# Expert weight rows dealt to partitions in 8 KB runs, with strided slices in the transposes that match them

## What is computed

```
for e in range(N_EXPERTS):
    h = jax.nn.silu(xf @ w_gate[e]) * (xf @ w_up[e])
    y = y + combine[:, e:e + 1] * (h @ w_down[e]).astype(jnp.float32)
```

## Time and profile before

| | |
|---|---|
| median of three executions | 643.84 us |
| profiled execution, span | 643.9 us |
| MoE on PE, from the first transpose of a gathered tile to the last matmul | 241.2 to 557.7 us |
| one step of the loop | 17.9 us |
| busy: PE, DVE, ACT, POOL | 92%, 80%, 56%, 31% |
| read from HBM, written | 147.90 MB, 14.41 MB |

### The profile page before, as it was taken

One profiled execution on the slowest core, in us unless ns is written; L12 is line 12 of the kernel. 1 busy time (PEld: TensorE's weight loads), 2 busy tenths in 40 slices (PEclk: granted clock), 3 DMA queues, 4 the chain that ended last, 5 costly groups with the idle time before them and its releaser, 6 DMA issues.

```text
span 643.9 us, 9840 instructions
## 1 busy us (share of the span) xinstructions
PE 593.1 (92%) x3432; PEld 512.1 (80%) x3432; DVE 512.3 (80%) x555; ACT 362.7 (56%) x369; POOL 198.7 (31%) x202
## 2 busy tenths in 40 slices
PE   3799999989999889799999999999999999459994
PEld 2799999968788777688888888888888888359993
DVE  4769998995633587889999999999999998387545
ACT  6712222426434526687777777778777877334343
POOL 8063635982000007422211222222221311122104
PEclk9799999979999899999999999999999999869997
DMA  9986221035131408699999999999999999480003
GB/s 255 282 255 242 66 67 66 1 140 183 57 152 66 148 30 254 248 397 394 398 396 385 389 381 362 383 379 371 387 386 366 378 376 326 154 294 3 1 1 147
DMA packets 79065, 153.99 MB, mean 239 GB/s; under 512 B 8411, under 2 KB 26419, under 8 KB 78579
## 3 DMA queue, kind: packets, MB, share of 16 engines
q1 hardware_dynamic: 71627, 138.98, 60.8%
q0 software_dynamic: 5520, 9.56, 4.0%
q10 hardware_dynamic: 1888, 5.05, 2.2%
HBM read 147.90 MB, written 14.41 MB: 252 GB/s over the span
## 4 chain that ended last, share of the span: by engine, by line
PE 70%; DMA 12%; DVE 5%; POOL 4%; ACT 3%; SPq 2%; issue 2%; POOLq 0%; ACTq 0%; DVEq 0%
PE pair L1626 19%; PE pair L1627 18%; PE pair L1628 18%; PE pair L1673 8%; DMA raw<-in_w_exp_gate 6%; PE pair L1637 3%; DMA raw<-in_w_exp_down 2%; ACT hi L826 2%; DVE lo L1174 2%; PE pair L1861 1%; DMA two<-normed,gidx 1%; SPq L459 1%; POOL h L681 1%; POOL h L683 1%; DMA two<-in_state_conv 1%
## 5 line engine op out<-in xcount | busy, mean ns | idle before, releaser
L1626 PE MATMUL pair<-hi,act_hi 128*128 128x512 f32 (+3 forms) x748 | 275.6, 369 | 7.2 <-DVE act_lo L1467 2.9
L1174 DVE TENSOR_TENSOR lo<-raw,hi 128x2048 fp32r<-128x2048 f32 x111 | 251.8, 2291 | 31.1 <-ACT hi L826 30.3
L1627 PE MATMUL pair<-lo,act_hi 128*128 128x512 f32 (+3 forms) x748 | 268.6, 359 | 0.0
L1628 PE MATMUL pair<-hi,act_lo 128*128 128x512 f32 (+3 forms) x748 | 268.6, 359 | 0.0
L826 ACT ACTIVATE hi<-raw 128x2048 fp32r<-128x2048 f32 x119 | 225.5, 1916 | 51.4 <-PE pair L1673 23.2
L1626 PEld LDWEIGHTS pair<-hi,act_hi 128*128 128x128 f32 (+1 forms) x748 | 139.5, 187 | 33.8 <-issue 5.7
L1628 PEld LDWEIGHTS pair<-hi,act_lo 128*128 128x128 f32 (+1 forms) x748 | 139.4, 186 | 22.3
L1627 PEld LDWEIGHTS pair<-lo,act_hi 128*128 128x128 f32 (+1 forms) x748 | 139.6, 187 | 19.1
L737 POOL DMA_INDIRECT pairs<-two,sidx x17 | 42.5, 2500 | 108.2 <-DVE two L1475 108.2
L1220 DVE SCALAR_TENSOR_TENSOR pair<-conv,vecs,pair 128x512 f32<-128x512 f32 x112 | 74.8, 746 | 0.0
L826 ACT ACTIVATE act_hi<-pair 128x1024 fp32r<-128x1024 f32 (+3 forms) x50 | 38.3, 782 | 58.5 <-PE pair L1637 33.3
(11 more groups left out here) (217 smaller groups left out, 512.3 us busy)
## 6 DMA issues: line engine op xcount, KB each, us to landing
raw<-in_w_exp_gate SPq DMA_DIRECT2D x34, 1024.0 KB, 10.5
raw<-in_w_exp_up SPq DMA_DIRECT2D x34, 1024.0 KB
raw<-in_w_exp_down SPq DMA_DIRECT2D x34, 1024.0 KB, 11.9
h<-in_x_prompt SPq DMA_DIRECT2D x8, 512.0 KB, 6.4
raw<-in_w_in SPq DMA_DIRECT2D x8, 512.0 KB, 12.0
raw<-in_w_in SPq DMA_DIRECT2D x4, 1024.0 KB, 9.1
raw<-in_w_out SPq DMA_DIRECT2D x4, 1024.0 KB, 4.9
raw<-in_w_ple_gate SPq DMA_DIRECT2D x4, 1024.0 KB
```

The source lines that it names most:

```text
L1174: nc.vector.tensor_tensor(lo[:, n % SPLIT, :], raw[:, n % RAW, :], hi[:, n % SPLIT, :].bitcast(F32), ALU.subtract).then_inc(lo_dve, 1)
L1626: mm(out_, x_hi, w_hi, start=start, stop=False)
L1627: mm(out_, x_hi, w_lo, start=False, stop=False)
L1628: return mm(out_, x_lo, w_hi, start=False, stop=stop)
```

## The change

The source of an expert's unit is viewed differently, so that partition p of a unit takes consecutive rows of the matrix: four for gate and up (rows 4p to 4p + 3 of the unit's 512), two for down. These are 8 KB in one piece. The unit is the same 1 MB of memory as before, in the same buffer, at the same place of SP's order. Chunk c of a gate or up unit now holds the rows 4p + c, so the token row must be cut in the same way: `dealt_rows` transposes, for chunk c, the elements 4n + c of the unit's half of the row, a slice whose elements are four floats (16 bytes) apart. For `hid` they are two floats (8 bytes) apart. The number, size and order of the transposes and matmuls stay as they were.

```diff
@@ unit_source
             if k < 4:
                 w = a["w_exp_gate"] if k < 2 else a["w_exp_up"]
-                w = w[0].rearrange("e (c p) n -> (e c) p n", p=P)
-                at = e * DC + (k % 2) * (DC // 2)
-                return w[bass.ds(at, DC // 2)].rearrange("c p n -> p c n")
-            w = a["w_exp_down"][0].rearrange("e (c p) n -> (e c) p n", p=P)
-            at = (e - 1) * CB + (k - 4) * 2
-            return w[bass.ds(at, 2)].rearrange("c p n -> p c n")
+                w = w[0].rearrange("e (u p c) n -> (e u) p (c n)", u=2, p=P)
+                return w[bass.ds(e * 2 + k % 2, 1)].rearrange("o p m -> (o p) m")
+            w = a["w_exp_down"][0].rearrange("e (u p c) n -> (e u) p (c n)", u=2, p=P)
+            return w[bass.ds((e - 1) * 2 + k - 4, 1)].rearrange("o p m -> (o p) m")
@@ load_unit
-                sp.dma_start(raw[:, n % RAW, :].rearrange("p (c n) -> p c n", c=src.shape[1]), src)\
-                  .then_inc(raw_in[n % RAW], 16)
+                to = raw[:, n % RAW, :]
+                if n < N_MOE or n >= N_GATE:
+                    to = to.rearrange("p (c n) -> p c n", c=src.shape[1])
+                sp.dma_start(to, src).then_inc(raw_in[n % RAW], 16)
...
@@ tensor
+            def dealt_rows(src, to, per):
+
+                dealt = src.rearrange("r (u n c) -> r u c n", n=P, c=per)
+                for i in range(src.shape[1] // P):
+                    ins = tr(to[:, i * P:(i + 1) * P], dealt[:, i // per, i % per, :], ident[:, :])
+                return ins
...
@@ transpose_gathered
-                transpose_rows(xg, P, pair[1]).then_inc(g_ps, 1)
+                dealt_rows(xg, pair[1], DC // 2).then_inc(g_ps, 1)
@@ transpose_hidden
-                for c in range(CB):
-                    ins = tr(bank[4][:, c * P:(c + 1) * P], hid[:, c * P:(c + 1) * P], ident[:, :])
-                ins.then_inc(t_ps, 1)
+                dealt_rows(hid, bank[4], CB // 2).then_inc(t_ps, 1)
```

More of the change, by code:

```diff
@@ L527, in _ @@
                     for i, name in enumerate(("w_exp_gate", "w_exp_up", "w_exp_down")):
-                        c = CB // 2 if i == 2 else DC // 2
-                        src = a[name][0].rearrange("e (c p) n -> (e c) p n", p=P)
+                        src = a[name][0].rearrange("e (u p c) n -> (e u) p (c n)", u=2, p=P)
                         for k in range(2):
@@ L534, in _ @@
                             sp.wait_ge(*low_done(n))
-                            sp.dma_start(raw[:, n % RAW, :].rearrange("p (c n) -> p c n", c=c),
-                                         src[bass.ds(e * 2 * c + k * c, c)].rearrange("c p n -> p c n")).then_inc(v_w[i], 16)
+                            sp.dma_start(raw[:, n % RAW, :],
+                                         src[bass.ds(e * 2 + k, 1)].rearrange("o p m -> (o p) m")).then_inc(v_w[i], 16)
                     wait_all(sp, (v_gu, j))
@@ L2021, in _ @@
                     wait_all(pe, (v_in, 16 * j))
-                    transpose_rows(xg, P, pair[1]).then_inc(v_gps, 1)
+                    dealt_rows(xg, pair[1], DC // 2).then_inc(v_gps, 1)
                     wait_all(pe, (v_gsb, j))
@@ L2030, in _ @@
                     wait_all(pe, (v_hid, j))
-                    for c in range(CB):
-                        ins = tr(bank[4][:, c * P:(c + 1) * P], hid[:, c * P:(c + 1) * P], ident[:, :])
-                    ins.then_inc(v_tps, 1)
+                    dealt_rows(hid, bank[4], CB // 2).then_inc(v_tps, 1)
                     wait_all(pe, (v_tsb, j))
```

## The result

The changed kernel takes 650.8 us (median of 17 runs, 647.25 to 652.15). The kernel before, on the same chips, takes 646.07 us (17 runs, 643.69 to 648.98). The ratio is 1.006 with a 95% interval of 1.0044 to 1.0076, so the change costs 3.9 us, 2.8 to 4.9 (the medians are 4.7 us apart). The forecast of "slower" holds; its size, 12.1 us, does not. The spans of the profiled executions are 643.9 us before and 649.3 us after, 5.4 us apart. Where both are on record, the time of an execution is 1.8 us above its span (651.14 against 649.3, 644.71 against 642.9), so the first profile of before is of an execution of about 645.7 us; that its span fell on the median of three times was chance. Since single executions of one kernel differ by some 5 us, two more of each kernel were profiled later, with spans of 642.9 and 644.4 us before, 648.8 and 648.6 after.

The account below looks back on a forecast made before the run. PE's own instructions were taken to bound the loop, with the loads hidden. 643.9 + 11.3 (strided transposes) + 1.5 (gather) - 0.7 (last down unit) = 656.0 us; the forecast's own range was 654 to 659, the wider one 643.5 to 661.

Parts of the forecast that it names:

- The forecast of "slower": Whole kernel: the changed kernel would be slower, given a chance of 0.61.
- The bound: MoE loop: PE's own instructions set the time, 17.92 us a step, and hide the loads' 15.7 us of every DMA engine.
- Theory C: Loads, a theory of the experiments: the earlier loads must be worth a microsecond or more somewhere.
- The step that failed: Transposes on PE: a weight load takes about 0.11 us without slack, so PE pays a strided read's cost, 0.10 us each.
- The term of 15 x 0.75 = 11.3 us: Strided transposes of gathered rows, steps 2 to 16: 0.75 us more a step on PE's path, with `hid` counted at nothing.
- the strides of the first two groups: Transposes of steps 0 and 1: their 1.5 us would be taken up by PE's 1.55 us wait at 272.41 us.
- The gather: Gather of step 2, for which PE waits: turns with 8 KB load packets make it 1.5 us later, between 0 and 5.
- the rival of the starved queue: POOL's queue in the loop: gathers land 16.2 us after issue, PE waits about a microsecond a step; 660 to 672 us, chance 0.04.
- The last down unit: Loop's end: the last down unit arrives in time, DVE starts earlier, PE gains 0.7 us, between 0 and 1.15.
- the rival of the free step: Strided transposes: the step costs a weight load nothing; 644.7 us, between 643.2 and 647, chance 0.37.

Follow-up runs that it names:

- half_low: Kernels before and after, each with half the products with the weights' low part left out on PE and half that part on DVE: 644.23 us before, 630.74 after.
- gather_early: Kernels before and after, each with POOL issuing the gather of step 2 four slot scatters earlier: 649.09 us before, 648.4 after.
- wide_strides: Changed kernel with doubled steps: gathered rows read with 32 bytes instead of 16, `hid` with 16 instead of 8: 649.81 us, ratio 1.0052.
- fill_after: Changed kernel with ten unused 128 x 512 matmuls on PE ahead of step 2's transposes: 648.7 us, ratio 1.0054.
- runs_alone: Changed kernel with its 8 KB loads but adjacent transposes: 648.29 us, ratio 1.0024.
- strides_alone: Kernel before with strided transposes only, its loads unchanged: 648.11 us, ratio 1.0026.
- early_peeled_after: Changed kernel with the earlier gather of step 2, and SP issuing step 2's six units before waiting for the slot lists: 646.12 us, ratio 0.9991.
- early_peeled_before: Kernel before with the earlier gather of step 2, and SP issuing step 2's six units before waiting for the slot lists: 641.42 us, ratio 0.9938.
- gather_early_after: Changed kernel with POOL issuing the gather of step 2 four slot scatters earlier: 648.4 us, ratio 1.0022.

## Why the prediction was wrong in size

*The bound* was read rightly: PE sets the loop before and after, and the loads are hidden behind it. But their packets were priced too low, from a window of 2.4 us: over the ten steps of the earlier trace rows queue q1 has 94.9% of the engines, 17.0 us a step where 15.7 was reckoned, and 16.4 after. Theory C fails in the whole kernel, and the pairs `half_low` and `gather_early` show why.

*The step that failed* is the one that said "So the load of 128 fp32 columns alone takes about 0.11 us, and a transpose has no slack over it: whatever a strided read costs the load, PE pays." The load did become longer, by 208 - 140 = 68 ns for the gathered rows, two thirds of the 100 ns taken (line 1405's 58 ns were on 80 elements, 93 on 128). But PE paid 0.009 us for it a transpose, not 0.10: the pitch went from 0.109 to about 0.12 us. The answer stood in the earlier trace rows: loads of 140 ns mean, begun 0.11 us apart, must overlap. The router's sixteen loads, which the prediction took to last 0.116 us each, say the same: they last 191 ns and are begun 0.116 us apart. A pitch is a rate, and a longer duration changes it only when there is no room left; at 188 ns (`wide_strides`) there still was. The term of 15 x 0.75 = 11.3 us measures 15 x 0.13 = 2 us, and it has `hid` in it, which I had counted at nothing because PE passes through 16 bytes fast enough; its loads went from 139 to 204 ns all the same. Nor did the wait at step 2 take up the strides of the first two groups: they put the gather's issue off by 0.17 us, which makes 2.1 in all. The Trainium skill's rule (SBUF — State Buffer, section SBUF: two separate sides: lines of 16 bytes, two or more hits for full bandwidth), by whose first half I had let `hid` go free, isn't borne out here: 8 and 16 byte steps make the load equally long, and 32 bytes less.

*The gather* was right in its mechanism and twice too large: 1.5 us forecast, 10.33 - 9.52 = 0.8 us of landing and the same of waiting measured (means of three). The turns can be seen in after, from 270 to 272.5 us, while the gather lands (queue: packets, MB, share of 16 engines):

```profile
q1 hardware_dynamic: 101, 0.70, 66.4%
q0 software_dynamic: 100, 0.35, 34.1%
```

One for one, as in the earlier trace rows, and each turn of q1 is now 0.664 x 16 x 2.5 / 101 = 263 ns against 84. The Trainium skill has the rule too (DMA: Bandwidth & Descriptors, section Queues, rings and completion order: an engine goes round the queues a packet at a time), and the trace agrees, at 101 to 100. In the loop the gathers and scatters of after land later too, at a median of 8.3 and 10.4 us over the ten steps where before has 7.5 and 8.6, and PE waits for none of them, as forecast: the rival of the starved queue fails.

*The clock* was in no term of the sum, which is the second step that failed. Behind the wait that was 0.8 us longer came a stretch of 3.41 us at half clock, 1.7 us more: twice what the longer landing itself cost. `fill_after` is what ties it to the wait.

*The last down unit* was forecast at -0.7 us and gave about -0.15. ACT then waited for PE's products and not for the load, and DVE's `act_lo` stayed the last to come:

```profile
549.29 1.92 ACT L825 ACTIVATE hi<-raw 128x2048 fp32r<-128x2048 f32 x1 [0.80 <-PE pair L1627]
...
554.94 0.77 PE L1625 MATMUL pair<-hi,act_hi 128*128 128x512 f32 x1 [2.54 <-DVE act_lo L1466]
```

PE's last wait is 2.54 us in place of the 2.93 of the earlier trace rows. But in the two further profiles of before that unit is not late either, ACT waits 0.80 us for PE as here, and PE's last wait is 2.59 us; in those of after it is 2.56. The term was built on a delay that one execution had.

*In sum*: 2.1 (strides) + 0.8 (gather) + 1.7 (clock at step 2) - 0.15 (last unit) = 4.45 us, where the table has 4.1 up to the head's products; the 0.35 between them is not explained. With 0.9 from head to gate rows the table has 5.0 of the 5.2 us between the profiles. By the profiled spans (649.3, 648.8, 648.6) the rival of the free step (644.7 us) was some 4 us too low and the forecast (656.0) 7 us too high: the rival's strides are nearer, and both lack the clock.

*Open* is the 0.9 us after the loop. Between 560 and 583 us the clock is at half for 17.1 us in all three profiles of after and in one of before (the one with 11.10 us), and for 13.7 us in the other two of before, so the difference is one more stretch of 3.4 us (11.10 against 9.75 us between two profiles of before). `runs_alone`, `fill_after` and `wide_strides`, which load as the changed kernel does, have 13.7 us: nothing shows that this part belongs to the change. Open too is why a few packets straggled in `strides_alone`, and why `early_peeled_after` is 4.7 us behind `early_peeled_before` at the median, when strides account for 2.1.

## What to carry to other kernels

Before a cost per instruction is put on the path, compare its duration with the pitch of its row: where the duration is the longer, instructions overlap, and a longer one may cost nothing. Larger runs save DMA time only where a load is waited for; compare a step of the loads alone with a step of the engine that hides them, since a lead of some buffers can hide a deficit for a while. Ask what each larger packet makes the other queues wait, and whether a short transfer that PE waits for is among them. And where a wait of TensorE becomes longer, look at the granted clock behind it: here 0.8 us of further waiting was followed by 1.7 us lost to the clock.

## What the runs showed of the hardware

- Weight loads of 128 fp32 columns take 139 to 140 ns in the mean when adjacent, 204 to 208 with steps of 8 or 16 bytes, and 188 with 32. The pitch of a row of transposes is 0.109, 0.12 and 0.11 us. Why the widest step is the cheapest of the three is not known.
- A wait of PE of 2.44 to 2.96 us at this place was followed by some 3.4 us at half clock in six profiles (three of after, `strides_alone`, `runs_alone`, `wide_strides`); waits of 1.55 to 1.93 us (three of before) and of 0.63 us (`fill_after`) were not. At other places the length of the wait does not sort them: ahead of step 0 waits of 2.16 to 2.49 us were not followed by half clock in nine profiles and one of 2.40 us was (`early_peeled_after`), and in step 1 the idle 1.77 us of PE were in `gather_early_after` and `early_peeled_after`, while 1.69 to 1.78 us there were not in twelve others.
- With DMA as the bound, 1 MB loads in 8 KB runs move 403 GB/s in the loop, and those in 2 and 4 KB runs 383.
